# Sample states of the mLSTM layer: one 1 MB transfer per head and sample through two slots, in place of two 512 KB transfers through four

## The reference, cut to what matters

```python
# C: 512x512 state; k, v, q: 512-vectors of the sample's token; a, i: gate scalars; n, m: normaliser, stabiliser
C_new = a * C + outer(i * k, v)                      # read 1 MB, written back 1 MB as C_sample
num   = q @ C_new                                    # 512-vector
h     = num / maximum(abs(q @ n_new), exp(-m_new))   # then output gate, layer norm, skip, z gate, w_out
```

## Time and profile before

| what | value |
|---|---|
| median of 3 executions | 1167.39 us (1164.23 to 1171.07) |
| profiled execution | 1168.19 us |
| its span, first to last instruction | 1166.5 us (1.7 us less than the execution) |
| mean granted TensorE clock | 0.958 |
| PE busy | 1067.0 us (91%) |
| DVE, ACT, POOL busy | 628.5, 364.6, 226.0 us |
| DMA traffic | 191.58 MB, mean 164 GB/s |
| state loads, 64 of 512 KB | median 5.8 us from issue to landing |
| state stores, 64 of 512 KB | median 6.2 us |

### The profile page before, as it was taken

How to read it: one execution, slowest core, us unless ns; L and a number is a source line. 1 busy time by engine, 2 the same in 40 slices (tenths; PEclk the granted TensorE clock), 3 DMA queues, 4 the chain that set the end, 5 groups by cost and what they waited for, 6 DMA issues and landing times. The chain is left out here.

```text
span 1166.5 us, 15189 instructions
## 1 busy us (share of the span) xinstructions
PE 1067.0 (91%) x5316; PEld 714.1 (61%) x5316; DVE 628.5 (54%) x1002; ACT 364.6 (31%) x669; POOL 226.0 (19%) x168
## 2 busy tenths in 40 slices
PE   5899999997796669999799999999999999996998
PEld 3677777774342369989643585447744684444776
DVE  4655555566286569996444444355346444456332
ACT  4434444333000133333433223521443133323210
POOL 5434443411010043432301111010201001100000
PEclk9999999998798969999899999999999999997999
DMA  9222223344675444545559921996269813973221
GB/s 244 73 80 66 63 85 90 91 163 162 203 263 190 145 63 151 161 156 176 176 172 327 302 92 54 316 350 140 92 215 339 247 55 118 331 255 146 72 73 74
DMA packets 145994, 191.58 MB, mean 164 GB/s; under 512 B 23714, under 2 KB 87058, under 8 KB 144366
## 3 DMA queue, kind: packets, MB, share of 16 engines
q1 hardware_dynamic: 130782, 157.05, 42.0%
q0 software_dynamic: 5808, 24.35, 6.3%
q10 hardware_dynamic: 9344, 9.39, 2.4%
HBM read 135.66 MB, written 55.22 MB: 164 GB/s over the span
## 5 line engine op out<-in xcount | busy, mean ns | idle before, releaser
L1872 DVE SCALAR_TENSOR_TENSOR state<-state,s_all,outer 128x1024 f32<-128x1024 f32 x64 | 81.4, 1284 | 102.1 <-DMA state<-in_state_C 72.8
L2061 PE MATMUL tok_ps<-w_og,hT 128*128 128x512 f32 (+1 forms) x320 | 121.5, 598 | 0.0
L629 PE MATMUL pj<-w_hi_a,h_hi_a 128*128 128x512 f32 x256 | 106.5, 416 | 5.6 <-POOL w_lo_a L454 5.6
L1733 ACT ACTIVATE outer<-v_bcast,k_cols 128x512 f32<-128x512 f32 x128 | 81.8, 710 | 93.3 <-DMA v_bcast<-keep_v_rows 92.0
L629 PE MATMUL pj<-w_lo_a,h_hi_a 128*128 128x512 f32 x256 | 101.2, 395 | 0.0
L629 PE MATMUL pj<-w_hi_a,h_lo 128*128 128x512 f32 x256 | 101.0, 395 | 0.0
L454 POOL TENSOR_TENSOR w_lo_a<-w_in,w_hi_a 128x1024 fp32r<-128x1024 f32 x32 | 77.9, 2456 | 88.9 <-ACT w_hi_a L329 49.8
L2061 PEld LDWEIGHTS tok_ps<-w_og,hT 128*128 128x128 f32 (+1 forms) x320 | 48.7, 169 | 70.1 <-issue 64.6
L1388 PE MATMUL xm_ps<-h_hi_c,w_col_hi 128*128 128x260 f32 x304 | 87.4, 288 | 0.0
L1995 PE MATMUL col_ps<-hT,shared 128*128 128x260 f32 x384 | 86.7, 384 | 0.0
L1388 PE MATMUL xm_ps<-h_hi_c,w_col_lo 128*128 128x260 f32 x304 | 85.8, 282 | 0.0
(11 more groups left out here) (303 smaller groups left out, 1847.0 us busy)
## 6 DMA issues: line engine op xcount, KB each, us to landing
state<-in_state_C SPq DMA_DIRECT2D x64, 512.0 KB, 5.8
out_C_sample<-state SPq DMA_DIRECT2D x64, 512.0 KB, 6.2
w_in<-in_a_w_in SPq DMA_DIRECT2D x64, 256.0 KB, 4.2
shared<-in_m_w_in SPq DMA_DIRECT2D x20, 512.0 KB, 4.8
k_pages<-in_cache_k SPq DMA_DIRECT2D x16, 512.0 KB, 7.6
w_og<-in_m_w_in POOLq DMA_DIRECT2D x4, 2048.0 KB, 11.2
v_bcast<-keep_v_rows SPq DMA_DIRECT2D x32, 256.0 KB, 6.5
shared<-in_m_w_in POOLq DMA_DIRECT2D x12, 512.0 KB, 4.8
```

The source lines that it names most:

```text
L629: last = nc.tensor.matmul(pj[:, t % 2, :], a, b[:, j, k, :, :].rearrange("p m d -> p (m d)"), start=(k == 0 and n == 0), stop=(k == KT - 1 ...
L1733: last = nc.scalar.activation(outer[:, g, d, :], vb[:, b % 2, :], ACT.Copy, scale=kc[:, 2 * g + d, b:b + 1])
L1872: nc.vector.scalar_tensor_tensor(out=state[:, k % 4], in0=state[:, k % 4], scalar=s_all[:, 0, ds(h, 1), b], in1=outer[:, g], op0=ALU.mult, ...
L2061: last = nc.tensor.matmul(tok_ps[out, u % 2, :], c.hT[:, k, t * P:t * P + p], wg[:, k, :], start=(k < sums), stop=(k >= KT - sums))
```

## The change

The slots become two of 1 MB. SP works by sample: it waits until both halves of sample b are new, stores the whole 1 MB, loads v of sample b + 2, waits for that same store and for PE's use of both halves, and loads sample b + 2 into the slot. Two samples, not three halves, are loaded ahead of head 0. DVE still works by halves, and waits for the whole sample's load before the first of them; PE and ACT are unchanged.

```diff
-        st_in = [m.sem(f"state_in{j}_d") for j in range(4)]
-        st_out = [m.sem(f"state_out{j}_d") for j in range(4)]
+        st_in = [m.sem(f"state_in{j}_d") for j in range(2)]
+        st_out = [m.sem(f"state_out{j}_d") for j in range(2)]
...
-            def half(arr, h, k):
-                b, g = divmod(k, 2)
-                return arr[b, ds(h, 1)].rearrange("a (g d p) e -> p g (a d) e", g=2, p=P)[:, g]
-
-            def load_state(h, k):
-                sp.dma_start(state[:, k % 4], half(io.state_C, h, k)).then_inc(st_in[k % 4], 16)
+            def whole(arr, h, b):
+                return arr[b, ds(h, 1)].rearrange("a (g d p) e -> p g (a d) e", g=2, p=P)
+
+            def load_state(h, b):
+                sp.dma_start(state[:, 2 * (b % 2):2 * (b % 2) + 2], whole(io.state_C, h, b)).then_inc(st_in[b % 2], 16)
...
-                for k in range(PIECES):
-                    sp.wait_ge(new_ready, PIECES * h + k + 1)
-                    sp.dma_start(half(io.C_sample, h, k), state[:, k % 4]).then_inc(st_out[k % 4], 16)
-                    if k % 2 and k // 2 + 2 < DEC:
-                        load_vb(h, k // 2 + 2)
-                    if not (last and k + 3 >= PIECES):
-
-                        if k > 0 or not isinstance(h, int) or h > 0:
-                            sp.wait_ge(st_out[(k - 1) % 4], 16 * (4 * h + (k - 1) // 4 + 1))
-                            sp.wait_ge(sn_used, PIECES * h + k)
-                        load_state(h if k + 3 < PIECES else h + 1, (k + 3) % PIECES)
-
-            for k in range(3):
-                load_state(0, k)
+                for b in range(DEC):
+                    sp.wait_ge(new_ready, PIECES * h + 2 * b + 2)
+                    sp.dma_start(whole(io.C_sample, h, b), state[:, 2 * (b % 2):2 * (b % 2) + 2]).then_inc(st_out[b % 2], 16)
+                    if b + 2 < DEC:
+                        load_vb(h, b + 2)
+                    if not (last and b + 2 >= DEC):
+                        sp.wait_ge(st_out[b % 2], 16 * (4 * h + b // 2 + 1))
+                        sp.wait_ge(sn_used, PIECES * h + 2 * b + 2)
+                        load_state(h if b + 2 < DEC else h + 1, (b + 2) % DEC)
+
+            for b in range(2):
+                load_state(0, b)
...
-                    dve.wait_ge(st_in[k % 4], 16 * (4 * h + k // 4 + 1))
+                    dve.wait_ge(st_in[b % 2], 16 * (4 * h + b // 2 + 1))
```

More of the change, by code:

```diff
@@ L1603, in _ @@
             for s in st_out:
-                sp.wait_ge(s, 16 * PIECES * M_HEADS // 4)
+                sp.wait_ge(s, 16 * DEC * M_HEADS // 2)
         @block.gpsimd
```

## The result

The changed kernel takes 1193.5 us (median of 4, 1187.5 to 1199.6) where the kernel before takes 1169.2 (median of 4 in all, 1164.2 to 1172.2): a ratio of 1.0205, 95% interval 1.017 to 1.024. It is slower by 24 us; the forecast was slower, by 17 on the profiled run (1185), with a range of 1170 to 1207. The profiled execution took 1193.83 us, its span 1192.1, 25.6 above that of before.

A forecast was written before the change was run, and what follows sets the result against it. The prediction held the stage bound by PE, with the DMA close behind. Sample 5's delays 9.9, sample 7's waits 5.7 and clock 1.7 made 17.3 us on the profiled 1168.2, 1185.5, forecast as 1185; range 1170 to 1207.

The forecast's parts named there:

- the wait before sample 5: PE before sample 5's second half: load 5 meets POOL's weights; delays 2.3, 2.9, 3.1 and 1.6 us, 9.9 in all.
- The cycle: SP's two slots, one store's landing to the next: 8.7 us against the 8.06 PE asks; the main term.
- fixed 2.6 us: Part of a state transfer independent of bytes, from a 512 KB load's 4.1 us less 1.5 for bytes.
- The load: A 1 MB state transfer alone: 2.6 us fixed plus 3.0 for bytes, 5.6 us.
- 0.1 us for SP's waking: In the cycle: SP's time to wake after a store has landed, before it issues the next load.
- Heads 1 to 3: Delays of sample 5's second half there: 2.9, 3.1 and 1.6 us, after 2.3 in head 0.
- the second rival: Weights catch the cycle earlier: at 320 GB/s a 9.3 us cycle, sample 5 late by about 5, 1203 us in all; chance 0.22.
- Issues at nothing: SP's queue: 128 state transfers become 64, costed at nothing because SP's own waits hide the issues.
- loads ahead at nothing: Start of a head: two samples ready instead of one and a half; nothing gained.
- Sample 7: Load 7 runs beside POOL's 1 MB; PE waits 1.9 us in all heads but the last, 5.7 us.
- Clock: PE at half clock after idling near the one-column matmuls: one more stretch, 1.7 us; bounds nothing or 6.8.
- The first rival: Large transfers cheap enough: 4.6 us per 1 MB alone, a 6.7 us cycle, no waits left, 1163 us; chance 0.13.

The follow-up runs named there:

- halves: Changed kernel's order of waits, but two transfers of 512 KB where it has one of 1 MB: 1186.9 us, 1.0156 of the kernel before.
- three slots: Changed kernel with three 1 MB slots; SP stores sample b, waits for the store of b - 1, loads b + 2: 1162.2 us, 0.9951 of the kernel before.
- the written-out loop: Changed kernel with only SP's loop over heads 1 and 2 written out, as a control: 1193.6 us, 1.0223 of the kernel before.
- 512 KB ones: Three 1 MB slots, SP waiting for the previous sample's store, each transfer cut into two of 512 KB: 1161.6 us, 0.9948 of the kernel before.
- the run with v on ACT and three slots: Changed kernel with three slots, SP still waiting for each own store, v of samples 2 to 7 loaded by ACT's queue: 1169.8 us, 1.0005 of the kernel before.
- the run with both gains: Changed kernel with three slots (SP waits for store b - 1) and POOL's 2 MB of weights moved to the head's end, heads 0 to 2: 1160.9 us, 0.9938.

## Why the prediction was right

The direction, the place (the wait before sample 5 in all four heads) and the mechanism hold: order and lead, much more than size, as the runs with halves and with three slots show. The sizes of the terms hold less well, and that the time fell into the range is in part luck.

- *The cycle*, forecast 8.7 us. In head 0 it is 8.8 and 8.9, and the start of sample 5's second half is 43.0 us after sample 0, forecast 42.7 as its end. But its parts are not those of the forecast. The load of the earlier trace rows had no empty queue: the DMA engines were as busy before its issue at 609.44 as behind it, so its 4.1 us give no fixed 2.6 us.

```profile
608.00:609.40 1.40, 1.40 (x10) 0.26 (x9) 0.00 (x0) 0.60 (x1) 0.00 (x0) 1.00 1.04 364
609.40:611.00 1.60, 1.60 (x4) 0.76 (x5) 0.81 (x1) 0.00 (x0) 0.00 (x0) 1.00 0.96 324
```

- *The load*, the step that failed: 5.6 us were forecast for each 1 MB. A store with nothing ahead of it took 4.6, and a load in the cycle, with v queued ahead of it and a store behind, 6.1 to 7.0. How much of that is v, which the forecast put at nothing, no run takes apart. No row gives the 0.1 us for SP's waking either; after the store issued at 614.44, which took 8.5 us, the load follows at once, at 622.97.
- *Heads 1 to 3*: the cycle is 9.1 to 9.7 there, so the term was mis-sized. The second halves start 2.6, 5.8, 5.1 and 5.3 us later than before in the four heads, 18.8, where 9.9 were forecast. This is the second rival's case. Its point is the landing of store 2 at 622, 21.8 us after sample 0; load 4, issued at that landing, stands 21.0 us after sample 0 in head 0, but 23.3, 22.4 and 23.8 in heads 1 to 3. There the weights meet store 3, and the next load comes 11.7 to 13.2 us later; sample 5 is late by about the 5 us that the rival gives.
- *Issues at nothing* and *loads ahead at nothing*: nothing in the traces speaks against it; the written-out loop, which saves some of SP's instructions, changed no time.
- *Sample 7*, forecast 1.9 us in three heads: there is no wait. Load 7 took 7.9, 9.3 and 8.8 us there, not 9.6, and PE asked for it 63.8, 66.6 and 64.9 us after sample 0, not 63.0, since more was lost before.
- *Clock*, forecast 1.7 us, bound 6.8: four stretches more are the bound, 6.8. Four of the six follow the wait at sample 5; two follow the one-column matmuls (in heads 1 and 3), as two did before (in heads 2 and 3). Part of a stretch falls before sample 5's second half, so only 4.4 us come on top of the 18.8.

On the profiled executions the forecast was 17.3 us and the loss is 25.6. The cycle took 8.9 us more than forecast and the clock 2.7; sample 7 took 5.7 less; 2.4 lie outside the sample parts, 1.8 of them ahead of the stage. The first rival (large transfers cheap enough) had the right price for a lone store, 4.6 us, and fell on the pair: in a cycle the two do not move at that rate. One reading was off without effect: PE's slices in the stage stand at 9 from the twenty-first to the thirty-sixth.

The Trainium skill's advice to batch transfers to 1 MiB ("DMA: Bandwidth & Descriptors", section "Bandwidth") brought no gain here: with three slots 1 MB transfers take 1162.2 us and 512 KB ones 1161.6. PE waits for states in neither, so these runs do not show whether the larger ones move faster. The fit that the prediction takes from the same page of the Trainium skill (section "Anatomy of one DMA") is stated there for transfers that GpSimd issues, and SP issues the states. Its estimate of 4.4 us for 1 MB is near the 4.6 of the lone store all the same; the 4.1 us that the prediction holds against it are, as said, not a lone transfer's.

Not settled: what decides on half-clock stretches. They come after waits of PE or behind the row of one-column matmuls; at that second place the run with v on ACT and three slots has one in three heads, without any wait before it, and the run with both gains has none. The run with v on ACT and three slots takes 8 us more than the three-slot runs in which SP waits for the store before its own; it has these three stretches and 5.8 us of PE's waits for the z weights, and no run took the two apart.

## What to carry to other kernels

Merging transfers into fewer slots changes two things besides the count: how much is loaded ahead, and what SP's queue stands behind. Work out the cycle of a slot (store, landing, load, landing, compute) against the pace of the engine that uses it, and keep one transfer queued while the issuing queue waits for another's landing. List also what else is issued behind that wait: a small load there can become the limit when the large ones no longer are.

## What was not expected of the hardware

A 1 MB store with nothing ahead of it lands in 4.6 us, but store and load of 1 MB together need 8.8 to 9.7 us a cycle. And v, 256 KB, made the first cycles of head 0 0.8 and 0.6 us longer on a second queue than behind the store on the first (the whole run 1204.6 against 1193.5 us): there it landed before the store that the cycle waits for.
